# Who adds the picked expert rows to the residual stream: VectorE or GpSimd

## The reference

```python
top_val, top_idx = lax.top_k(logits, TOP_K)
top_w = jax.nn.softmax(top_val, axis=-1)
combine = jnp.sum(one_hot(top_idx, N_EXPERTS) * top_w[..., None], axis=-2)
out = jnp.zeros_like(h)
for e in range(N_EXPERTS):
    out = out + combine[..., e:e + 1] * _swiglu(h, w_gate[e], w_up[e], w_down[e])
...
h = h + _moe_swiglu(...)
```

## Time and profile before

| | |
|---|---|
| Median of 3 runs | 1472.76 us (1471.87 to 1474.74) |
| Profiled execution | 1469.46 us, its span 1467.6 us |
| PE busy | 1424.5 us, 97% |
| DVE busy | 1135.4 us, 77% |
| ACT busy | 999.9 us, 68% |
| POOL busy | 42.3 us, 3% |
| Memory traffic | 447.53 MB, mean 305 GB/s |

### The profile page before, as it was taken

One profiled execution on the slowest core, in us unless ns is written; L12 is line 12 of the kernel. 1 busy time (PEld: TensorE's weight loads), 2 busy tenths in 40 slices (PEclk: granted clock), 3 DMA queues, 4 the chain that ended last, 5 costly groups with the idle time before them and its releaser, 6 DMA issues.

```text
span 1467.6 us, 19843 instructions
## 1 busy us (share of the span) xinstructions
PE 1424.5 (97%) x7503; PEld 1216.1 (83%) x7503; DVE 1135.4 (77%) x865; ACT 999.9 (68%) x823; POOL 42.3 (3%) x71
## 2 busy tenths in 40 slices
PE   6999999999999899999999999999999999999997
PEld 6887899998897788888888888888888888888775
DVE  4466544445467798988888888888888888888997
ACT  4786443344676577777777777777777777777775
POOL 4100000000100100000000000000000000002000
PEclk9999999999999899999999999999999999999999
DMA  9834555554543499999999999999999999999993
GB/s 363 293 115 147 169 180 193 163 195 144 180 144 112 166 371 384 383 386 393 377 370 391 378 363 395 389 364 390 377 363 391 395 378 379 391 378 371 393 372 110
DMA packets 188128, 447.53 MB, mean 305 GB/s; under 512 B 7568, under 2 KB 9752, under 8 KB 188080
## 3 DMA queue, kind: packets, MB, share of 16 engines
q1 hardware_dynamic: 182928, 429.94, 80.5%
q0 software_dynamic: 3856, 12.67, 2.4%
q10 hardware_dynamic: 1296, 4.26, 0.7%
HBM read 436.35 MB, written 10.49 MB: 304 GB/s over the span
## 4 chain that ended last, share of the span: by engine, by line
PE 88%; DVE 6%; ACT 4%; issue 2%; DMA 1%; ACTq 0%; SPq 0%; DVEq 0%
PE ps L1393 83%; ACT whi L535 2%; DVE wlo L919 2%; PE ps L1757 2%; DMA raw<-in_w_in_dram 1%; PE ps L1540 1%; PE ps L1412 1%; DVE y L941 0%; PE ps L1727 0%; ACT L545 0%; PE ps L1724 0%; DVE y L1104 0%; DVE qkc L987 0%; PE ps L1525 0%; PE ps L1544 0%
## 5 line engine op out<-in xcount | busy, mean ns | idle before, releaser
L919 DVE TENSOR_TENSOR wlo<-raw,whi 128x2048 fp32r<-128x2048 f32 x405 | 925.8, 2291 | 265.4 <-ACT whi L535 263.8
L535 ACT ACTIVATE whi<-raw 128x2048 fp32r<-128x2048 f32 x405 | 777.0, 1919 | 379.2 <-PE ps L1393 363.3
L1393 PE MATMUL ps<-whi,xT_hi 128*128 128x512 f32 x1056 | 417.5, 395 | 2.3 <-DVE wlo L919 2.1
L1393 PE MATMUL ps<-wlo,xT_hi 128*128 128x512 f32 x1056 | 411.9, 390 | 0.0
L1393 PE MATMUL ps<-whi,xT_lo 128*128 128x512 f32 x1056 | 411.2, 389 | 0.0
L1393 PEld LDWEIGHTS ps<-whi,xT_hi 128*128 128x128 f32 x1056 | 198.4, 188 | 43.5 <-issue 3.7
L1393 PEld LDWEIGHTS ps<-wlo,xT_hi 128*128 128x128 f32 x1056 | 198.2, 188 | 42.2
L1393 PEld LDWEIGHTS ps<-whi,xT_lo 128*128 128x128 f32 x1056 | 198.5, 188 | 38.8
L1393 PE MATMUL ps<-whi,hid_hi 128*128 128x512 f32 (+1 forms) x536 | 210.9, 393 | 0.8 <-DVE hid_lo L1221 0.8
L1393 PE MATMUL ps<-whi,hid_lo 128*128 128x512 f32 (+1 forms) x536 | 208.7, 389 | 0.0
L1393 PE MATMUL ps<-wlo,hid_hi 128*128 128x512 f32 (+1 forms) x536 | 208.7, 389 | 0.0
(11 more groups left out here) (243 smaller groups left out, 728.4 us busy)
## 6 DMA issues: line engine op xcount, KB each, us to landing
raw<-in_moe_w_gate_dram SPq DMA_DIRECT2D x112, 1024.0 KB, 7.1
raw<-in_moe_w_up_dram SPq DMA_DIRECT2D x112, 1024.0 KB, 7.4
raw<-in_moe_w_down_dram SPq DMA_DIRECT2D x112, 1024.0 KB, 7.0
raw<-in_w_in_dram SPq DMA_DIRECT2D x28, 1024.0 KB, 5.8
raw<-in_ffn_w_gate_dram SPq DMA_DIRECT2D x10, 1024.0 KB, 5.0
raw<-in_ffn_w_up_dram SPq DMA_DIRECT2D x10, 1024.0 KB, 5.1
raw<-in_ffn_w_down_dram SPq DMA_DIRECT2D x10, 1024.0 KB, 4.8
raw<-in_w_out_dram SPq DMA_DIRECT2D x8, 1024.0 KB, 4.9
```

The lines of the kernel that those rows point to most:

```text
L535: act.activation(whi[:, i % NSPLIT, :], raw[:, i % NRAW, :], ACT.Copy).then_inc(hi_ready, 1)
L919: dve.tensor_tensor(wlo[:, i % NSPLIT, :], raw[:, i % NRAW, :], whi[:, i % NSPLIT, :].bitcast(F32), ALU.subtract).then_inc(lo_ready, 1)
L1393: ins = pe.matmul(acc, lhs, rhs, start=start and m == 0, stop=stop and m == 2, skip_group_check=True)
```

## The change

VectorE no longer calls `add_picked`. GpSimd does the work with eight instructions behind its indirect DMAs: four products `picked *= pick_w` in place, two sums of the two choices of a token tile, and two additions into `h`. Its first waits are for all four fetches (`picked_in`) and for the weights (`pick_w_ready`, which the instruction that writes `pick_w` now sets). Each later instruction waits on a semaphore for those whose result it reads. `picked_added` counts to two instead of four, and `add_job` waits for that.

```diff
@@ gpsimd, behind the indirect DMAs
+            pool.wait_ge(picked_in, 16 * 2 * TT)
+            pool.wait_ge(pick_w_ready, 1)
+            for t in range(TT):
+                for c in range(2):
+                    pool.tensor_scalar(picked[t][c], picked[t][c], pick_w[:, t, c:c + 1], None, ALU.mult
+                                       ).then_inc(picked_scaled, 1)
+            for t in range(TT):
+                pool.wait_ge(picked_scaled, 2 * t + 2)
+                pool.tensor_tensor(picked[t][0], picked[t][0], picked[t][1], ALU.add
+                                   ).then_inc(picked_summed, 1)
+            for t in range(TT):
+                pool.wait_ge(picked_summed, t + 1)
+                pool.tensor_tensor(h[:, t, :], h[:, t, :], picked[t][0], ALU.add
+                                   ).then_inc(picked_added, 1)
@@ add_job
-                dve.wait_ge(picked_added, 4)
+                dve.wait_ge(picked_added, TT)
@@ slots_of_results
-                own(dve.tensor_tensor(pick_w[:], rt[:, 15, :, 6:8], rt[:, 11, :, 0:2], ALU.mult))
+                dve.tensor_tensor(pick_w[:], rt[:, 15, :, 6:8], rt[:, 11, :, 0:2], ALU.mult
+                                  ).then_inc(pick_w_ready, 1)
@@ vector
-            def add_picked(k):
-                t, c = k // 2, k % 2
-                dve.wait_ge(picked_in, 16 * 2 * TT)
-                if c:
-                    dve.wait_ge(picked_added, k)
-                dve.scalar_tensor_tensor(h[:, t, :], picked[t][c], pick_w[:, t, c:c + 1], h[:, t, :],
-                                         ALU.mult, ALU.add).then_inc(picked_added, 1)
@@ rest_of_job
-                    if with_table and i in (24, 27, 30, 33):
-                        add_picked((i - 24) // 3)
```

More of the change, by code:

```diff
@@ L277, in trunk @@
         picked_added = sem("picked_added")
+        pick_w_ready = sem("pick_w_ready")
+        picked_scaled = sem("picked_scaled")
+        picked_summed = sem("picked_summed")
         scatT_ps = sem("scatT_ps")
```

## The result

The changed kernel takes 1482.89 us (median of 4 runs, 1480.13 to 1483.4), against 1473.08 us before on the same chip. The ratio is 1.0066, 95% interval 1.0053 to 1.0078: slower by 9.7 us, between 7.8 and 11.5. The forecast was 7.5 us more, 1480.3 us, with a range to 1485.5.

The account below looks back on a forecast made before the run. TensorE was taken as the bound, delayed by VectorE in the last job. Holds of 12.6 us less 1.4 and 2.5 hidden leave 8.7; less 1.2 gained, +7.5 us: 1472.8 to 1480.3 us, range 1471.5 to 1485.5.

Parts of the forecast that it names:

- Removed: 1.2 us: Last job's two blocks with four fused additions on VectorE return to 16.78 us, gaining 0.59 + 0.62 = 1.2 us.
- The exclusion holds both ways: Last job: GpSimd instructions reading SBUF and VectorE splits with two SBUF inputs wait for each other, a whole instruction long.
- Rivals 1 and 2: VectorE never held: 1471.6 us, chance 0.20; likewise, but GpSimd needs instruction-long gaps and delays `add_job`: 1478.4 us, chance 0.04.
- Rival 3, seldom turns: Held both ways, but GpSimd gets in only in gaps every 4 to 6 us; about 1475.5 us, chance 0.15.
- The port time of 12.6 us: GpSimd's eight instructions in the last job: four sums 8.8 us plus four products 3.8 us, at most 18.4 us.
- the bound of 2.3 us above: Upper bound for one GpSimd product on 128x1024, from the two-input rate; 0.95 us was taken.
- What hides: Of 12.6 us, 1.4 under the lead and 2.5 beside VectorE's idle time and PSUM reads; 8.7 us reaches TensorE.
- TensorE's lead: TensorE has two pieces (5.60 us) against 4.21 us to refill a split buffer; a single VectorE delay to 1.4 us is free.
- The end of GpSimd's work near 1390 us: Last job: eight GpSimd turns from about 1358.5 us end near 1390 us, inside blocks where VectorE already delays TensorE.
- my sign for it, a block of 20 us or more: Transposes (L1757) 20 us or more apart in one or two last-job blocks after 1358 us would show the prediction right.

Follow-up runs that it names:

- no additions: The kernel before without the weighted additions of the picked rows on any engine; `add_job` waits for the fetches only; ratio 0.9988 to before.
- The memsets: The changed kernel with its eight GpSimd instructions replaced by twelve memsets of 128x1024 into the same buffers, additions left out; ratio 0.9997 to before.
- eight half sums: The change with GpSimd instructions cut to 512 columns, sums unpaced, or waiting for chosen splits (paced, bunched); ratios 1.0066, 1.0012 and 1.0021 to before.
- sums-only kernel: The change without its four products: GpSimd does the two sums and two additions into `h` on unscaled rows; ratio 1.0053 to before.
- Products only: The change with only the four products on GpSimd; VectorE adds the scaled buffers to `h` at the places of before; ratio 1.0021 to before.
- unpaced halves: The change with each GpSimd instruction cut into two of 512 columns, same order, no added waits; ratio 1.0066 to before.
- the kernel that starts after the table: The change with one more wait: GpSimd begins only when the overflow table is made (i = 20); ratio 1.0046 to before.

## Why the prediction was right, and where its sizes were off

**Removed: 1.2 us.** Right. The two blocks went from 17.37 and 17.40 to 16.78 and 16.81 us, and the kernel with no additions gives the same.

**The exclusion holds both ways.** Right, and shown. The earlier trace rows had GpSimd waiting for a split; the changed kernel has both in one trace: sums of 4.45 us instead of 2.2, and splits of 4.48 us instead of 2.29. The memsets show that it takes reads by GpSimd, and that its writes do not matter. The Trainium skill, "SBUF — State Buffer", section "Who interferes with whom", says both (two SBUF inputs against a GpSimd instruction that reads; not against one that only writes), and the traces agree with both. That the exclusion lasts for a whole instruction, as the prediction cites it, fits the sums (2.2 us of work, up to 2.2 us of hold) and not the products (2.85 us of work, 0.7 to 0.9 us of hold); there the measurement decides. Rivals 1 and 2 are out by the stretched splits; `add_job` never waited for GpSimd, which was done at 1392.3 us.

**Rival 3, seldom turns.** Out: Where GpSimd had to wait it got its turn at the end of the split in progress, in each case but one. The exception is the second product, asked for at 1365.22 us, 0.4 us before a split ended: the next split went first, and the product came one split later. Why it lost this one turn stays open.

**The port time of 12.6 us.** The total was nearly right, by luck in one part. The sums were taken at 2.2 us and hold VectorE 2.2 us. The products were taken as 0.95 us of work and hold; they are 2.85 us of work and 0.7 to 0.9 us of hold. True holds are thus 3.1 + 8.8 = 11.9 us. Had I known the true duration and taken it as the hold, I would have had 20.2 us of holds and a forecast 7.6 us too high against this one. The trace of before had the operation on eight columns only, and the bound of 2.3 us above was too low for its duration.

**What hides.** I put 2.5 us beside idle time and PSUM reads and 1.4 us under TensorE's lead, 8.7 us left. Of 11.9 us of holds VectorE shows 10.7, so 1.2 us were hidden there; TensorE paid 9.7 us, so about 1.0 us fell under the lead. The covers were sized too large by 1.3 and 0.4 us and the holds by 0.7, which makes the 1.0 us between the forecast (7.5) and the distances (8.5). That the holds came too close for the lead to be rebuilt between them is my reading; the trace shows only that VectorE had no idle time from 1360.2 to 1401.0 us.

**The end of GpSimd's work near 1390 us** (1392.3) and the two blocks hit were right; my sign for it, a block of 20 us or more, was met by both (24.4 and 21.8).

## What to carry to other kernels

Count elementwise work moved to GpSimd as work for VectorE too, wherever VectorE's instructions have two SBUF inputs and are near the bound: here 5.1 us on VectorE that cost 1.2 became GpSimd instructions that held VectorE 10.7 us. Measure cover in time and place, not in total: a delay under the lead of the consumer (1.4 us here) is free once, and the same eight half sums cost 1.3, 2.8 or 8.4 us by where they met VectorE's list. Before moving work to another engine, look for a gap in the list of its own: two of the four additions fitted behind the last split, the other two one to a block, at no cost.

## What the runs showed of the hardware that was not expected

**TensorE's clock fell behind a long stall.** The granted clock of TensorE in the changed kernel, per microsecond (length, busy, PEclk, DMA share, GB/s), around the stall of 2.88 us that ended at 1377.48 us:

```profile
1377.00:1378.00 1.00, 0.52 (x2) 1.00 1.05 387
1378.00:1379.00 1.00, 1.00 (x4) 0.66 1.05 387
1379.00:1380.00 1.00, 1.00 (x4) 0.50 1.08 406
1380.00:1381.00 1.00, 1.00 (x4) 0.50 1.02 401
1381.00:1382.00 1.00, 1.00 (x5) 0.63 0.95 377
1382.00:1383.00 1.00, 1.00 (x6) 1.00 0.95 197
```

It is at 0.50, the 1.2 GHz level, for 3.4 us in sum and then back at 2.4 GHz. In the sums-only kernel TensorE stood still for 6.28 us, and from 1380 to 1386.7 us the clock was at 0.50. Its TensorE timeline, two of its microseconds, and VectorE behind it:

```profile
1380.95 0.80 PE L1396 MATMUL ps<-whi,hid_hi 128*128 128x512 f32 x1 [6.28 <-DVE hid_lo L1233]
```

```profile
1384.00:1385.00 1.00, 1.00 (x4) 0.50 0.90 332
1387.00:1388.00 1.00, 1.00 (x6) 1.00 0.93 324
```

```profile
1388.48 2.29 DVE L931 TENSOR_TENSOR wlo<-raw,whi 128x2048 fp32r<-128x2048 f32 x1 [2.59 <-ACT whi L547]
```

There slow matmuls held up ScalarE and so VectorE, which sat idle 2.59 us in the middle of the backlog: I take this for the reason why sums only cost 10.2 us for 7.7 us of holds (two splits at 7.93 us instead of 4.5, two small instructions at 2.35 and 2.29 us instead of 0.16). Products only has the same picture (a stall of 2.88 us, 0.50 from 1378 to 1381 us, VectorE idle 1.73 us), and pays 3.9 us for 3.1.

What the drop costs depends on whether the slow matmuls are on the chain that ended last. In time order (start us, us, what), the chain of products only, then two pieces of that of the changed kernel:

```profile
1376.90 4.64 PE ps L1403 x12
```

```profile
1377.42 3.78 DVE wlo L936
1396.68 3.05 PE ps L1401 x12
```

In products only the twelve slow matmuls are on the chain and take 4.64 us, where twelve at full clock take 3.05 in the changed kernel: 1.6 us. In the unpaced halves, at 0.50 from 1393 to 1399.8 us, twelve took 4.91 us on the chain: 1.9 us. In the changed kernel the chain runs on VectorE while the clock is low, and VectorE is never idle there, so in this trace the drop cost nothing; no run tried that by itself. The other three executions of the changed kernel had mean clocks of 0.986 to 0.989 against 0.990 in the traced one, and took 2.5 to 3.3 us longer. Whether the clock cost them time is open, as they have no trace.

The length of a stall does not tell alone whether the clock falls. In the kernel that starts after the table no stall is longer than 2.0 us, and its clock stays at 1.00. But the longest stall of the changed kernel, the 3.14 us that ended at 1396.68 us, was not followed by a drop either:

```profile
1397.00:1398.00 1.00, 1.00 (x6) 1.00 0.49 37
```

What sets it apart from the one of 2.88 us stays open.

**A GpSimd product with a weight per partition** takes 2.85 us on 128x1024, longer than a sum of two tensors, but holds a VectorE instruction with two SBUF inputs for less than a third of that (0.69 to 0.88 us). Why the hold is so short, and the half products (1.56 us where nothing is in their way) hold it for 0.5 us at most and mostly not at all, stays open.
